# A macaron SwiGLU block with a conv and state-space mixer on one core: the mixer's input projection as two-by-two block products

## The reference

```
proj = h @ w_in                                    # 1024 x 5632
gate_b, gate_c, v, u, glog_a, glog_b = split(proj) # 1024, 1024, 1024, 512, 1024, 1024 columns
y_a = (gate_b * short_conv(gate_c * v, conv_w)) @ w_conv_out      # causal, 3 taps, per channel
s = s5_ssm(u, ...) + d_skip * u                    # 32 groups of 16 channels, 64 complex states each
s = gelu(s);  s = s * sigmoid(s @ w_glu);  y_b = s @ w_ssm_out
out = (sigmoid(glog_a) * y_a + sigmoid(glog_b) * y_b) @ w_out
```

## Time and profile before

| | |
|---|---|
| three runs | 2208.27, 2206.03, 2205.05 us; median 2206.03 |
| profiled execution | 2204.14 us, span of its instructions 2202.3 us |
| granted TensorE clock, mean | 0.993 of full speed |
| busy in the span | PE 2156.3 us (98%), weight loads 1778.0, DVE 1066.8 (48%), ACT 586.4 (27%), POOL 1151.8 (52%) |
| matmuls | 9890 |
| DMA | 194.68 MB, mean 88 GB/s |

### The profile page before, as it was taken

One profiled execution on the slowest core, in us unless ns is written; L12 is line 12 of the kernel. 1 busy time (PEld: TensorE's weight loads), 2 busy tenths in 40 slices (PEclk: granted clock), 3 DMA queues, 4 the chain that ended last, 5 costly groups with the idle time before them and its releaser, 6 DMA issues.

```text
span 2202.3 us, 27524 instructions
## 1 busy us (share of the span) xinstructions
PE 2156.3 (98%) x9890; PEld 1778.0 (81%) x9890; DVE 1066.8 (48%) x1197; ACT 586.4 (27%) x887; POOL 1151.8 (52%) x828
## 2 busy tenths in 40 slices
PE   6999999999999999999999989999999999999998
PEld 4778888888888788888888878887888888888887
DVE  6964445363644896334352544337633333334256
ACT  4622231313233510000101221115421323223234
POOL 1565564737374354544444575543853746465561
PEclk8999999999999999999999999999999999999999
DMA  7132424151411442323232154411111111212111
GB/s 287 58 115 80 131 68 155 47 170 57 152 39 44 145 124 74 105 66 105 73 95 86 53 191 162 125 48 29 58 39 58 58 58 38 76 38 67 29 58 77
DMA packets 234345, 194.68 MB, mean 88 GB/s; under 512 B 22996, under 2 KB 207456, under 8 KB 233120
## 3 DMA queue, kind: packets, MB, share of 16 engines
q1 hardware_dynamic: 210624, 154.52, 22.8%
q10 hardware_dynamic: 23648, 39.20, 5.6%
HBM read 167.34 MB, written 25.17 MB: 87 GB/s over the span
## 4 chain that ended last, share of the span: by engine, by line
PE 89%; DVE 3%; POOL 2%; ACT 2%; SPq 1%; issue 1%; DMA 1%; ACTq 0%; DVEq 0%; POOLq 0%
PE unit_a L818 13%; PE unit_b L818 13%; PE unit_d L1164 10%; PE unit_b L1164 9%; PE unit_c L958 9%; PE unit_d L958 9%; PE unit_c L1164 7%; PE unit_a L1164 7%; PE unit_d L818 2%; PE unit_c L818 2%; PE unit_c L1184 1%; PE unit_d L1184 1%; ACT t_plain L1409 1%; SPq L525 1%; DVE unit_c L1832 1%
## 5 line engine op out<-in xcount | busy, mean ns | idle before, releaser
L707 POOL TENSOR_TENSOR w_high<-raw,ones 128x512 fp32r<-128x512 f32 x136 | 192.6, 1416 | 375.3 <-PE unit_b L818 154.8
L746 POOL TENSOR_TENSOR w_low<-raw,w_high 128x512 fp32r<-128x512 f32 x200 | 272.8, 1364 | 208.0 <-ACT w_high L1486 192.1
L716 POOL TENSOR_TENSOR w_low<-raw,w_high 128x512 fp32r<-128x512 f32 x96 | 140.9, 1470 | 285.8 <-ACT w_high L1443 285.8
L1486 ACT ACTIVATE w_high<-raw 128x512 fp32r<-128x512 f32 x200 | 126.3, 632 | 399.5 <-PE unit_b L1164 139.5
L709 POOL TENSOR_TENSOR w_low<-raw,w_high 128x512 fp32r<-128x512 f32 x136 | 196.4, 1444 | 10.7
L746 POOL TENSOR_TENSOR w_low<-w_mixed,w_high 128x512 fp32r<-128x512 f32 x80 | 107.4, 1343 | 67.2 <-ACT w_high L1486 62.1
L818 PE MATMUL unit_a<-h_high,w_high 128*128 128x512 f32 x400 | 123.7, 390 | 0.5 <-ACT u_all L1625 0.5
L2054 DVE TENSOR_TENSOR fg_two<-fg_one,unit_b 128x512 f32<-128x512 f32 x60 | 41.3, 688 | 170.3 <-PE unit_b L1164 170.2
L818 PE MATMUL unit_b<-h_high,w_high 128*128 128x512 f32 x400 | 123.6, 390 | 0.0
L818 PE MATMUL unit_a<-h_low,w_high 128*128 128x512 f32 x400 | 123.2, 389 | 0.0
L818 PE MATMUL unit_b<-h_low,w_high 128*128 128x512 f32 x400 | 123.2, 389 | 0.0
(11 more groups left out here) (444 smaller groups left out, 5269.7 us busy)
## 6 DMA issues: line engine op xcount, KB each, us to landing
raw<-in_w_a SPq DMA_DIRECT2D x66, 512.0 KB, 4.5
raw<-in_w_b SPq DMA_DIRECT2D x66, 512.0 KB, 3.9
raw<-in_w_in SPq DMA_DIRECT2D x44, 512.0 KB, 3.8
ada_ring<-in_w_ada SPq DMA_DIRECT2D x84, 256.0 KB, 3.3
ada_first<-in_w_ada SPq DMA_DIRECT2D x8, 1024.0 KB, 14.3
sg_kept<-s ACTq DMA_DIRECT2D x16, 512.0 KB, 2.6
s<-sg_kept ACTq DMA_DIRECT2D x16, 512.0 KB, 3.4
ada_ring_last<-in_w_ada SPq DMA_DIRECT2D x28, 256.0 KB, 3.5
```

The costliest lines, as they stand in the source:

```text
L707: pool.tensor_tensor(high, raw[:, r, rows, :], one, ALU.mult).then_inc(high_split, 1)
L716: pool.tensor_tensor(low_, plain, high.bitcast(F32), ALU.subtract).then_inc(f.operand_low, 1)
L746: pool.tensor_tensor(low_, weight_plain(PRODUCTS[q][0], slots), high.bitcast(F32), ALU.subtract).then_inc(f.operand_low, 1)
L1486: act.activation(operand((RING[n] + q) % 4)[0], weight_plain(PRODUCTS[q][0], slots), ACT.Copy).then_inc(f.operand_high, 1)
```

## The change

40 of the 44 tiles of w_in are taken in 20 pairs as two-by-two block products (`N_MIX` = 20); the four u tiles stay slabs. The order of the pairs is `MIXER`: for each t two gate pairs, then c, v and b; in the last t one gate pair, c, v, b, and the second gate pair. So the matrices are 0 g, 1 g, 2 c, 3 v, 4 b, 5 g, 6 g, 7 c, 8 v, 9 b, 10 g, 11 g, 12 c, 13 v, 14 b, 15 g, 16 c, 17 v, 18 b, 19 g. The first state-space step of the four u tiles (`chunks_in`) stands behind matrices 2, 6, 10 and 14, the second (`chunks_out`) behind 5, 8, 12 and 16. All matrices use the one bank set of units A and B, since C and D serve the state-space part. Loops over the turns become straight code.

TensorE, `mixer_matrix`:

```diff
+                for q, (_, b_name, to, anew) in enumerate(PRODUCTS):
+                    pe.wait_ge(mixer.operand_low, o + q + 1)
+                    if m == 0:
+                        ...
+                    elif q == 0:
+                        pe.wait_ge(corner, m)
+                    elif q == 2:
+                        pe.wait_ge(mixer.evacuated, 5 * (m - 1) + 4)
+                    elif q == 3:
+                        pe.wait_ge(mixer.evacuated, 5 * m)
+                    if not anew and to == 0:
+                        pe.wait_ge(mixer.first_copied, m + 1)
+                    elif not anew:
+                        pe.wait_ge(mixer.evacuated, 5 * m + to)
```

```diff
+                    summed(a_["a21"], a_["a11"], a_["a21"], ALU.subtract, 1)
+                    summed(mixer_mixed, a_["a22"], a_["a21"], ALU.subtract, 2)
+                    operand_low(0)
+                    summed(a_["a11"], mixer_mixed, a_["a11"], ALU.add, 3)
+                    operand_low(1)
+                    summed(mixer_mixed, a_["a12"], mixer_mixed, ALU.subtract, 4)
+                    for q in range(2, N7):
+                        operand_low(q)
```

DVE, the order of a matrix (the multiplications for v and b pairs only; the corner is ACT's, with the sigmoid, for g and c):

```diff
+                between(m, 0)
+                dve.wait_ge(mixer.first_copied, m + 1)
+                out_of(1, 2, u2, u2, bank(0, 1))
+                between(m, 1)
+                out_of(2, 3, to[1, 1], u2, bank(0, 2), 1)
+                between(m, 2)
+                out_of(3, 4, to[1, 1], to[1, 1], bank(0, 3), 2)
+                multiply(1, 1, 3, 1)
+                between(m, 3)
+                if conv:
+                    dve.wait_ge(corner, m)
+                    dve.wait_ge(mixer.operand_used, o + 5)
+                    times(0, 0, bank(0, 0)).then_inc(corner, 1)
+                out_of(4, 6, to[0, 1], u2, bank(0, 2), 1)
+                multiply(0, 1, 4, 2)
+                between(m, 4)
+                out_of(5, 7, to[1, 0], u2, bank(0, 3), 4 if conv else 1)
+                multiply(1, 0, 5, 3)
+                between(m, 5)
```

`between(m, n)` holds what was DVE's set-up and `scan`, `kernels` and `conv`, cut in pieces:

```diff
+                if (m, n) == (0, 0):
+                    powers(1)
+                    powers(2)
+                elif (m, n) == (0, 1):
+                    powers(4)
+                elif (m, n) == (0, 2):
+                    all_powers()
+                elif (m, n) == (0, 3):
+                    input_factor()
+                elif (m, n) == (0, 4):
+                    inputs()
+                elif (m, n) == (1, 0):
+                    outputs_table()
+                    turns_begin()
+                ...
+                elif (m, n) == (3, 0):
+                    doubled(turn_low, 8, 8)
+                elif (m, n) == (3, 2):
+                    turns_high()
+                ...
+                elif MIXER[m][0] == "b" and n < 2:
+                    taps(MIXER[m][1], n)
+
+                for pieces, where in ((kernel_ba_real, ((1, 1), (5, 3), (8, 5), (12, 3))),
+                                      (kernel_ba_imag, ((1, 3), (5, 4), (9, 4), (12, 4))),
+                                      (kernel_ca_real, ((2, 0), (6, 0), (10, 0), (13, 0))),
+                                      (kernel_ca_imag, ((2, 2), (6, 2), (10, 2), (13, 3))),
+                                      (turn_table, ((3, 3), (7, 0), (11, 0), (15, 0))),
+                                      (turn_back, ((4, 4), (7, 2), (11, 2), (15, 2))),
+                                      (recurrence, ((5, 0), (7, 4), (11, 4), (15, 4))),
+                                      (turn_forth, ((5, 2), (8, 0), (12, 0), (16, 0)))):
```

ACT, the order around the high parts of a matrix:

```diff
+                for q_ in range(N7):
+                    weight_high(m, q_)
+                    if m == 0 and q_ == 1:
+                        keep_u(3, u_late[:, 1, :], 8)
+                        load_u(0)
+                    if m == 0 and q_ == 2:
+                        ...
+                        act.activation(unit_pw[:, 1, 1, :], q[1][:, :], ACT.Sin).then_inc(trig_act, 1)
+                        act.activation(unit_pw[:, 0, 1, :], q[2][:, :], ACT.Sin).then_inc(trig_act, 1)
+                    if m > 0 and q_ == 1:
+                        first_corner(m - 1)
+                    ...
+                    if q_ == 3:
+                        if m - 1 in CHUNKS_IN:
+                            weights_out(CHUNKS_IN[m - 1])
+                        if m > 0:
+                            keep_tile(m - 1, 0)
+                            keep_tile(m - 1, 1)
+                        if m - 1 in CHUNKS_OUT:
+                            chunk_out(CHUNKS_OUT[m - 1])
+                        ...
+                    if q_ == 4:
+                        first_copy(m)
```

SP: the u tiles are loaded before the parameters, and the parameters wait for the end of the first FFN and no longer for the start of its last down product:

```diff
-            sp.wait_ge(first_ffn.operand_used, LAST.down_op)
+            ...
+            sp.wait_ge(first_ffn.operand_used, LAST.down_op + KD)
             load_parameters()
```

More of the change, by code:

```diff
@@ new lines, in first_corner @@
+            def first_corner(m):
+                kind = MIXER[m][0]
+                if kind not in ("gate", "c"):
+                    return
+                act.wait_ge(corner, m)
+                act.wait_ge(mixer.operand_used, mixer_op(m) + 5)
+                if kind == "gate":
+                    act.activation(stage_block(0, 0), bank(0, 0), ACT.Sigmoid).then_inc(corner, 1)
+                    sigmoid(m, 1, 1, 3)
+                else:
+                    act.activation(gv_block(0, 0), bank(0, 0), ACT.Copy).then_inc(corner, 1)
@@ L1697, in _, with gelu @@
-            mix(0, first=True)
-            with act.Fori(1, NT - 1) as t:
-                mix(t)
-            mix(NT - 1, last=True)
+                    return
+                for n in range(NT):
+                    act.dma_start(u_all[:, n, :], u_kept[n]).then_inc(u_back, 16)
+                for n in range(NT - 1):
+                    act.dma_start(y_all[:, n, :], y_kept[n]).then_inc(y_loaded, 16)
+            def gelu(t):
+                act.wait_ge(s_sum, t + 1)
+                own.then(act.activation(u_all[:, t, :], u_all[:, t, :], ACT.Gelu_apprx_tanh))
@@ L1702, in _ @@
+            first_corner(N_MIX - 1)
+            for r in range(2):
+                keep_tile(N_MIX - 1, r)
+            act.wait_ge(s_sum, NT)
             for stage_ in range(2):
@@ L2282, in scan_setup, with tables @@
                     doubled(turn_high, half, n)
-                own.then(dve.memset(states[:, :, :, 0:1], 0.0))
-            def kernels(t):
-                if not (isinstance(t, int) and t == 0):
-                    dve.wait_ge(ssm_full, 1 + 4 * t)
+            def tables(t):
                 four = "p d (t k) -> p t k d"
-                powers = [pw[:, part, :, :].rearrange(four, k=4)[:, t, :, :] for part in range(2)]
                 late = [pv[:, part, :, :].rearrange(four, k=4)[:, t, :, :] for part in range(2)]
+                powers_ = [pw[:, part, :, :].rearrange(four, k=4)[:, t, :, :] for part in range(2)]
@@ L2372, in conv @@
-                if not (isinstance(t, int) and t == 0 and e == 0):
-                    dve.wait_ge(z_saved, 16 * (2 * t + e))
-                own.then(dve.tensor_scalar(taps[:, :], steps[2], tap(2), None, mul))
+                    return column(vt[:, CW + k * KD:CW + k * KD + KD], 2 * t + r)
+                own.then(dve.tensor_scalar(stage[r][:, :], steps[2], tap(2), None, mul))
                 for k in (1, 0):
-                    own.then(dve.scalar_tensor_tensor(out=taps[:, :], in0=steps[k], scalar=tap(k),
-                                                      in1=taps[:, :], op0=mul, op1=add))
@@ L2412, in _ @@
+            angles()
+            for m in range(N_MIX):
+                mixer_matrix(m)
+            dve.wait_ge(z_saved, 16 * KD)
             here = at["glu"]
@@ L2419, in _ @@
             here = at["ssm_out"]
-            with dve.Fori(0, 2) as i:
+            for i in range(2):
                 for u in range(4):
```

764 lines of the change are left out of this document (485 added, 279 removed).

## The result

The changed kernel takes 2219.43 us (median of four runs, 2217.19 to 2219.51), the kernel before 2205.54 beside it: ratio 1.0059, 95% interval 1.0047 to 1.0071. The forecast was 2188. The changed kernel's profiled execution has a span of 2217.6 us (before 2202.3).

A forecast was written before the change was run, and what follows sets the result against it. The prediction took TensorE's matmuls to bound the mixer. Removed matmuls (-54.4 us) and the other terms summed to -17.9: 2186 us against the profiled 2204.1, and 2188 as the median. Range 2164 to 2222, the forecast's own 2175 to 2201.

The forecast's parts named there:

- DVE becomes the bound: Rival: evacuations wait behind DVE's SBUF pieces, each POOL operation in the burst paid in full; 2223 us, chance 0.26.
- Its own signs: Mixer: TensorE busy below 99%, idle before products 5, 6 or 0 through DVE; DVE near 340 us; wrong if over 475.
- Removed matmuls: Mixer: two slabs become seven products of 12 matmuls, 19.04 us for 21.76; twenty pairs, -54.4 us.
- Start of matrix 0: Matrix 0 could start at 791.3; late operands for products 1 and 2 cost 2 us, bounds 0 and 5.
- Tables: Table pieces on DVE in matrices 0 and 1 make evacuations late: 11 us, bounds 8 and 20.
- Matrix 3: turns_high and turn_table on DVE delay matrix 3's evacuations: 8 us, bounds 3 and 16.
- Taps: Taps on DVE before evacuation 2 of matrices 4, 9, 14, 18: 2.5 us each, 10 in all.
- turn_forth, turn_back, recurrence: Pieces of 3.9, 3.9 and 4.7 us in slots with slack, one late: 3 us, bounds 0 and 12.
- Clock: One TensorE stall, the 4.8, near enough to 5.67 us to bring half clock: 2.7 us, bounds 0 and 13.
- ACT: 16 DMA issues on ACT delay high part 4 in three state-space steps: 1 us in all, 0 to 4.
- SP and the end: Later parameter loads hidden; at the end ssm_out's operand 1.9 us earlier, a last evacuation costing 0.7: -1.2 us.

The follow-up runs named there:

- loads_late: all_parts with the eight DMA issues loading the next row tile's chunks moved behind a matrix's sixth high part on ACT; 2165.05 us, 0.9806 to the kernel before.
- again: The changed kernel run once more, unedited; 2218.09 us, 1.0051 to the kernel before.
- dve_small: Changed kernel with DVE's tables, turning and scans of turns 1 to 3 and all taps on one column or sixteen; 2191.88 us, 0.9932.
- final_two: loads_late with transposes before the statistics again and the table pieces of matrices 0 to 3 at other places; 2167.47 us, 0.9825.
- taps_psum: Changed kernel with taps' copy and scaling on ACT into PSUM, DVE's additions reading it, row tile 1's behind evacuation 2; 2198.17 us, 0.9961.
- all_parts: Changed kernel with turning, scans, taps and kernel tables' first products through PSUM, table pieces moved, statistics before transposes; 2173.27 us, 0.9847.
- turns_psum: Changed kernel with the turned inputs, the scans' output and a product of turn_forth in PSUM, same instructions; 2204.88 us, 1.0001 to the kernel before.

## Why the prediction was wrong

Rival "DVE becomes the bound" came in: losses of 55.6 us would have used up the gain, and idle time (44.5), half clock (16), small gaps (5.8) and the later start (4.6) took 70.9. The forecast's mechanism and this rival's are one, late evacuations behind DVE's SBUF pieces; what failed is the size of three terms, the taps, the turning and scans, and the clock. Its own signs came up: the mixer took over 475 us, TensorE waited for DVE before products 5, 6 and 0, and DVE was busy for 374 us, not 340. Term by term:

- *Removed matmuls, -54.4:* right, 9650 for 9890. But the mixer took 482.9 us, 7.9 more than 414.5 + 44.5 + 16, and the sum had no term for such small gaps. 2.1 of it was there before (471.0 us for 40 x 10.88 + 33.7), so 5.8 is new. loads_late keeps 6.6 of this kind, 1.8 of them the first state-space step at half clock. Where the rest comes from stays open.
- *Start of matrix 0, 2:* TensorE waited 2.4 for the low part, but matrix 0 began at 795.9, not 791.3. 1.0 us is older than the norm, and 3.4 were half clock in that execution (*again*).
- *Tables, 11:* 6.4 + 2.0 = 8.4 us. *Matrix 3, 8:* 6.0 + 0.6. Both sums were near, partly by luck: for matrix 3 the parts had been 3 (product 6) and 5 (the next matrix), and in matrices 0 and 1 they had been 4.8, 3.1 and 3. The pieces had been priced at their lengths in the trace before, where POOL worked beside them.
- *Taps, 10:* 17.7 us. **This step failed first.** The prediction had DVE out at 16.8 us with every POOL instruction paid in full, 3.2 late, and then took 2.5 a matrix. In matrix 4 TensorE could go on 17.8 us after the matrix's start, 4.0 late: the taps took 12.7 us instead of 6.9, and they began at 3.6 instead of 1.4, since DVE was still behind from matrix 3 and a multiplication before them took 1.58 us for 0.69.
- *turn_forth, turn_back, recurrence, 3:* 9.3 us, the stalls of matrices 5, 6, 8 and 11. I had eight scans at 4.7 us; at 0.97 each they take 7.7.
- *Clock, 2.7:* **the second failure, and the largest.** I let one stall be "near enough" to 5.67 us. In both profiles of the changed kernel nine stalls of the mixer, from 6.4 us down to 1.98 and 2.72, were each followed by 6 to 12 matmuls at half clock, at once or 1 us later; those of 1.96 us and less were not. Some 78 matmuls in each paid 16 us, 1.8 a stall. The length alone doesn't decide: in dve_small a stall of 1.89 us was followed by half clock, in final_two one of 1.98 and in taps_psum two of 2.42 and 2.66 were not.
- *ACT, 1:* nearly hidden in this kernel, since DVE was later; 3.2 us once DVE was cured (all_parts).
- *SP and the end, -1.2:* exact, 938.8 us from the mixer's end to the end of the span for 940.0.

Taps 7.7, turns 6.3, clock 13.3, start 5.0 and gaps 5.8, less 2.6 (tables), 1.4 (matrix 3) and 1.0 (ACT), make 33.1; -17.9 + 33.1 = 15.2, and the span grew by 15.3. The rule named beside the rival, the Trainium skill's "SBUF — State Buffer", SBUF: two separate sides (the ports DVE and GpSimd share are held by one of them for its whole instruction), agrees with turns_psum: 0.405 against 0.97 us for a scan by moving its operands to PSUM. That rival should have had more weight than 0.26: the text ahead had worked out a shared demand of 401 to 451 us against 414.5.

## What to carry to other kernels

Before giving DVE and GpSimd more work in the same stretch, count DVE's instructions that read SBUF alone, each at its length plus what it may wait for a POOL instruction beside it, and read the sum against each deadline, not against the stretch. Copies and scalings with one tensor belong to them (0.28 us became 0.91, and 0.75 became 1.56); the evacuations, with an operand in PSUM, do not (0.69 throughout). Then look for idle PSUM: the same change went from 0.6% slower to 1.9% faster, and 40 of these 55 us came with the scans, turns, taps and table products that got an operand there (ACT's share of the taps and their new place included). Price a stall of TensorE at its length plus the half clock that may follow.

## What the hardware showed that I had not expected

A DVE instruction on SBUF alone can wait out the POOL instruction beside it even if it has 48 columns (0.21 us became 1.30, POOL's took 1.26); with an input in PSUM it keeps 0.405 (scan) or 1.29 us (addition of 1024 columns). ACT's activation with a scale column may write 1024 columns to PSUM in 1.1 us beside both. And the same code after the same gap of 2.2 us ran 32 transposes in 3.59 us in one execution and 2.16 in another (*again*), and the norm's stretch in 34.2 and 30.8: one profile is not enough for a term of that size.
